# The first two blocks' front made in the projection's last token block, and the forget gates read one turn later

## What is computed

```python
h = rms_norm(x, norm_pre) * (1.0 + scale) + shift
q, k, v, f_logit, z_rwkv, p_pool, g = jnp.split(h @ w_in, IN_IDX, axis=-1)
# RWKV-7, before its scan over the tokens:
zf = zf + (token_shift(zf) - zf) * mu
r, k, v, wd, ad = jnp.split(zf, RWKV_IDX, axis=-1)
log_w = -DECAY_SCALE * jax.nn.sigmoid(w0 + jnp.tanh(wd) @ w2)
a = jax.nn.sigmoid(a0 + ad @ a2)
kk = (k * k_k).reshape(B, S, RWKV_HEADS, HEAD_DIM)
kk = kk / jnp.maximum(jnp.linalg.norm(kk, axis=-1, keepdims=True), 1e-12)
k = k * (1.0 + (a - 1.0) * k_a)
# attention: log_f = log_sigmoid(f_logit + f_bias), cum = cumsum(log_f)
y = jnp.concatenate([y_fox, y_rwkv, y_pool], axis=-1) * silu(g)
x = x + gate * rms_norm(y @ w_out, norm_post)
```

## Time and profile before

| | us |
|---|---|
| median of three runs | 3571.12 (3542.68 to 3572.24) |
| profiled execution | 3542.35 |
| its span | 3540.6 |
| TensorE matmuls busy | 3298.0 (93%) |
| VectorE busy | 2428.2 (69%) |
| ScalarE busy | 1965.7 (56%) |
| GpSimd busy | 1785.6 (50%) |

### The profile page before, as it was taken

One profiled execution on the slowest core, in us unless ns is written; L12 is line 12 of the kernel. 1 busy time (PEld: TensorE's weight loads), 2 busy tenths in 40 slices (PEclk: granted clock), 3 DMA queues, 4 the chain that ended last, 5 costly groups with the idle time before them and its releaser, 6 DMA issues. The chain is left out here.

```text
span 3540.6 us, 90103 instructions
## 1 busy us (share of the span) xinstructions
PE 3298.0 (93%) x31944; PEld 2282.0 (64%) x31944; DVE 2428.2 (69%) x4339; ACT 1965.7 (56%) x3745; POOL 1785.6 (50%) x2083
## 2 busy tenths in 40 slices
PE   6788999999999995999999899999999999979998
PEld 6783489459549742888888466566666666644444
DVE  5797756326533334788775889899899988965454
ACT  2444544325432234577774677677777777753333
POOL 2376400410230043254544798889889889852222
PEclk9898999999999997899998899999999999989999
DMA  7387435344444542232223202022020220215555
GB/s 317 129 303 254 167 128 190 131 149 159 159 143 152 169 155 82 63 86 79 65 53 74 52 16 59 10 56 59 9 58 10 57 58 7 60 70 190 188 185 178
DMA packets 247420, 401.09 MB, mean 113 GB/s; under 512 B 85549, under 2 KB 198916, under 8 KB 231844
## 3 DMA queue, kind: packets, MB, share of 16 engines
q1 hardware_dynamic: 223627, 383.75, 34.0%
q10 hardware_dynamic: 22880, 11.54, 1.3%
q0 software_dynamic: 480, 0.14, 0.1%
HBM read 272.77 MB, written 122.59 MB: 112 GB/s over the span
## 5 line engine op out<-in xcount | busy, mean ns | idle before, releaser
L2732 ACT ACTIVATE p<-psc,seam,sc 128x512 f32<-128x512 f32 (+3 forms) x1152 | 848.6, 743 | 283.1 <-PE psc L2793 270.2
L2711 POOL TENSOR_TENSOR plo<-p 128x512 f16<-128x512 f32 (+2 forms) x864 | 905.5, 1076 | 72.7 <-ACT p L2732 71.5
L2834 DVE TENSOR_REDUCE seam<-pm 128x1 f32<-128x512 f32 (+3 forms) x1152 | 703.5, 637 | 92.4 <-PE pm L1396 80.6
L646 PE MATMUL bank<-h,ring 128*128 128x512 f16 x2688 | 598.4, 381 | 4.5 <-DVE u L990 4.5
L651 PE MATMUL bank<-ring,h 128*128 128x128 f16 x8064 | 468.2, 222 | 25.5 <-ACT c L818 12.3
L646 PEld LDWEIGHTS bank<-h,ring 128*128 128x128 f16 x2688 | 264.1, 98 | 343.1 <-issue 43.0
L651 PEld LDWEIGHTS bank<-ring,h 128*128 128x128 f16 x8064 | 464.7, 99 | 27.0 <-issue 13.0
L1165 POOL CAST stage<-c 128x512 f16<-128x512 f32 x64 | 47.2, 738 | 767.5 <-DVE c L1006 767.5
L3036 PE MATMUL pz<-wo,yh 128*128 128x512 f16 x1024 | 305.6, 380 | 3.1 <-DVE yl L3068 3.1
L2864 DVE TENSOR_TENSOR plo<-p 128x512 f16<-128x512 f32 (+1 forms) x288 | 288.1, 1000 | 0.0
L1000 DVE TENSOR_TENSOR c<-bank,u 128x512 f32<-128x512 f32 x168 | 115.7, 689 | 249.3 <-PE bank L646 171.0
(11 more groups left out here) (430 smaller groups left out, 6837.2 us busy)
## 6 DMA issues: line engine op xcount, KB each, us to landing
ring<-scratch_ws SPq DMA_DIRECT2D x52, 1792.0 KB, 7.9
scratch_z<-stage SPq DMA_DIRECT2D x72, 256.0 KB, 3.1
scratch_ws<-h SPq DMA_DIRECT2D x10, 1792.0 KB, 6.9
y<-scratch_y SPq DMA_DIRECT2D x35, 512.0 KB
g<-scratch_g SPq DMA_DIRECT2D x35, 512.0 KB
xr<-in_x SPq DMA_DIRECT2D x34, 512.0 KB, 6.1
scratch_g<-stage SPq DMA_DIRECT2D x64, 256.0 KB, 6.2
scratch_qk<-stage SPq DMA_DIRECT2D x64, 256.0 KB, 2.6
```

Of the source, the lines that this page charges most:

```text
L646: t = nc.tensor.matmul(bank[b][:], m.ring[:, slot, l, bo, k, :], hh[:, side, r, ao, k, :], start=fresh and first, stop=last, skip_group_ch ...
L2711: nc.gpsimd.tensor_tensor(plo[:, k % NP, 0:w], p32[:, k % NP, 0:w], hi[:, 0:w], ALU.subtract)\
L2732: nc.scalar.activation(p32[:, k % NP, 0:w], psc[k % 2][:, 0:w], ACT.Exp, bias=xb[:, u, b, x // 4:x // 4 + 1], scale=m.sc[:, 0:1]).then_inc ...
L2834: nc.vector.tensor_reduce(mx[:, s, t, q:q + 1], pm[g][:, 0, 0:w], AX.X, ALU.max).then_inc(pm_d.sem, 1)
```

## The change

1. `h` is now two tensors, `h0` and `h1`. `h0` is kept to the attention's end, and the buffers of the front (before in `seam`) are carved from it, with `wa`, `vec` and two of the four buffers of `ar`; the other two of `ar` and `zv` are tensors of the recurrence.
2. The front's functions move, with their semaphores, into `block_front`, which both stages call. In the projection's last token block (turn FIRST = 297 opens it) the fronts of blocks 0 and 1 are made, beginning at turns FIRST + 29 and FIRST + 52. SP loads parameters and both z blocks in turn FIRST + 3. `logits` go to `ptr`, `kk_means` to `pf`.
3. `recur` makes fronts only for blocks 2 and up; `decay_sums` and the two matmuls before it come after the scores of block 0.
4. `forget` moves one turn on, behind the two last z shifts.

```diff
+        BEGIN = (29, 52)
+        def front_at(g, after):
+            r = g - FIRST - after
+            return BEGIN.index(r) if r in BEGIN[0:m.fronts] else None
...
@@ SP, project
+                    if g == FIRST + 3:
+                        sp.wait_ge(mm, FREE)
+                        fr.load_parameters(sp, a)
+                        for s in range(NC):
+                            sp.wait_ge(sent[s], 16 * (2 * TILES // NC))
+                        for b in range(m.fronts):
+                            fr.load_z(sp, b)
...
@@ TensorE, project, behind the turn's product
+                    b = front_at(g, 2)
+                    if b is not None:
+                        pe.wait_ge(m.f.par, 96)
+                        pe.wait_ge(f_out, NSB)
+                        if b:
+                            pe.wait_ge(m.f.gates_d.sem, b)
+                            pe.wait_ge(m.f.kss_d.sem, b)
+                        fr.logits(pe, b, (ptr[0][:], ptr[1][:]))
+                        fr.kk_means(pe, b, pf[:])
...
@@ ScalarE, project: tanh, kk_squares after 0 turns; gates, k_factor, norm_guard after 3; kk_inverse, exps after 6
+                    b = front_at(g, 5)
+                    if b is not None:
+                        fr.centred_sums(act, b)
+                        nc.scalar.preload_act_table_set(EXP_LN)
+                        fr.kk_log(act, b)
...
@@ VectorE, project: running_sums after 4, kk_unit after 7, operands after 8 (GpSimd: 5 and 8)
-                    if at is not None:
-                        if at[1] == 0:
-                            forget(at[0])
-                        elif at[2] == 1:
+                    if sub(g - 1) is not None and sub(g - 1)[1] == 0:
+                        forget(sub(g - 1)[0])
+                    if at is not None and at[1]:
+                        if at[2] == 1:
                             first_sum(at[0], at[1])
...
@@ recur, on each engine
-                    if there(n + 3):
-                        gates(n + 3)
+                    if FRONT <= n + 3 < BLOCKS:
+                        fr.gates(act, n + 3, bank)
...
@@ VectorE, recur
-                chain(nc.vector.memset(onesf[:], 1.0))
-                chain(nc.vector.memset(ls[:], 0.0))
-                decay_sums()
                 dve.wait_ge(cst, 2)
...
+                    if n == -2:
+                        decay_sums()
+                    if FRONT <= n + 3 < BLOCKS:
+                        fr.running_sums(dve, n + 3)
```

More of the change, by code:

```diff
@@ L1206, in _ @@
                         weight_sums(production(g, 0))
+                    b = front_at(g, 5)
+                    if b is not None:
+                        fr.k_new(pool, b)
+                    b = front_at(g, 8)
+                    if b is not None:
+                        fr.a_and_r(pool, b)
+                        fr.decay_between(pool, b)
+                        fr.r_k(pool, b)
 def persistent(nc, ctx):
@@ L1535, in recur @@
         pp_mm, pp_d = count("pp_mm", 1), count("pp_d", 1)
-        npar, nlate = 6, 11
+        nlate = 11
+        FRONT = m.fronts
         plan = m.plan
@@ L2075, in _ @@
                         state_decayed(n + 1, 0)
-                    if there(n + 4):
-                        tanh(n + 4)
-                        kk_squares(n + 4)
+                    if FRONT <= n + 4 < BLOCKS:
+                        fr.tanh(act, n + 4)
+                        fr.kk_squares(act, n + 4)
             @block.tensor
@@ L2124, in turn @@
                     g.then_inc(tr_mm.sem, 1)
-                def logits(b):
-                    past(pe, tanh_d, b, 1)
-                    past(pe, b_d, b - 1, 1)
-                    for k in range(2):
-                        for j in range(2):
-                            hs = rows(j)
-                            g = mm(bank[j][:, k * W:(k + 1) * W], wa[hs, k, :], zf[hs, b % 2, 4, :], start=True, stop=True)
-                    g.then_inc(wa_mm.sem, 1)
-                def kk_means(b):
-                    past(pe, ksq_d, b, 1)
-                    past(pe, b_d, b - 1, CB)
-                    mm(bank[2], m.headmean[:], ksq[:].rearrange("p k t -> p (k t)"), start=True, stop=True)\
-                        .then_inc(kk_mm.sem, 1)
                 def pool_product(b):
```

460 lines of the change are left out of this document (279 added, 181 removed).

## The result

The changed kernel takes 3537.3 us in the median of 20 runs (3517.2 to 3561.4), beside 3557.3 us for the kernel before in 20 runs of the same comparison (3542.7 to 3573.6). The ratio is 0.9937, with a 95% interval of 0.992 to 0.9954: 16 to 28 us less. The forecast was 3512 us. The measured time lies in its range (3494 to 3553), 25 us above its number. The profiled execution of the changed kernel took 3541.76 us (span 3540.1, mean granted clock 0.956), only 0.6 us less than that of before (3542.35 us).

The account below looks back on a forecast made before the run. TensorE bounds the projection; a chain through every engine and twice through HBM bounds the recurrence's first 90 us. Terms -7.2 - 6.2 + 4.4 - 21.4 = -30.4 from 3542.35 give 3512 us, range 3494 to 3553.

Parts of the forecast that it names:

- The stops, -7.2 us: Projection block starts: with forget gates later, three TensorE waits for copies shrink from 3.67 to 1.27 us, -7.2 us.
- The clock at these starts, -6.2 us: Three projection block starts: shorter stops leave TensorE's clock at 1.00, saving the slow stretches behind them, -6.2 us.
- The rival that the clock falls at the starts all the same (0.13): Projection block starts: clock still falls despite shorter stops, so 6.2 us are not gained, 3518 us; chance 0.13.
- Two fronts on TensorE, +4.4 us: Projection's last block: front matmuls for two blocks add 1.13 + 1.08 us each on TensorE, unhidden, +4.4 us.
- The rival of a front that waits for ScalarE (0.12): Projection's last block: a front matmul waits for ScalarE and the clock falls after it, +10 us, 3522; chance 0.12.
- The opening, -21.4 us: Recurrence's opening: block 0's scores start at once, so the chain through the first inverse ends earlier, -21.4 us.
- its rival: Recurrence's opening: HBM round trips run slower beside the loads, cutting the gain to 15 us, 3518 us; chance 0.10.
- The sum: Whole kernel: stops, clock, fronts and opening together, -7.2 - 6.2 + 4.4 - 21.4 = -30.4 us.
- What it was set against: Whole kernel: the sum was applied to the profiled execution's 3542.35 us, not the shown median of 3571.12 us.
- the lower as my number: Whole kernel: of two supposed run levels, the lower gives 3512 us; the upper, 3541 us, stays within the range.
- The slower rival's argument: Recurrence's first steps stay at low clock, 3552 us, chance 0.03; against it, clock returned after 16 us of solid work.

Follow-up runs that it names:

- e1: Kernel before with only the forget gates moved one turn later, behind the last z shifts; 3554.7 us, ratio 0.9979.
- e10: Changed kernel with 96 useless matmuls in recurrence steps 11 to 14, but only block 0's front made in the projection; 3513.9 us.
- e5: Kernel before with 96 matmuls of no use on TensorE in recurrence steps 11 to 14; 3538.1 us, ratio 0.9941.
- e2: Changed kernel with the forget gates put back at their old turn, so the fronts alone; 3533.7 us, ratio 0.9937.
- e4: Changed kernel with 96 matmuls of no use on TensorE in recurrence steps 11 to 14; 3507.3 us, ratio 0.9843.
- e3: Changed kernel run once more, unaltered, for a second profile; 3532.9 us, ratio 0.9924.
- e6: Changed kernel with 90 matmuls of no use on TensorE at the recurrence's opening, ahead of its first product; 3538.4 us, ratio 0.9933.
- e11: Changed kernel with 28 matmuls of no use, only at the small waits of recurrence steps 13 and 14; 3534.3 us.

## Why the prediction was off, by its own steps

- **The stops, -7.2 us: right.** Three waits of 1.3 us stand where three of 3.7 were.
- **The clock at these starts, -6.2 us: right, and 1.5 of it lost again elsewhere.** The clock is 1.00 at all three. In e1 the distances shrank by 3.5, 4.1 and 4.6 us, 12.2 in all, so 5.0 are the clock's where 6.2 were counted. (The second start was misread: by the earlier trace rows its slow stretch lasts from inside 786.5 to 787.0 to the end of 789.5 to 790.0, 3.4 us and not 2.9. With that, stop and clock make some 5.0, 4.1 and 4.7 us.) What is missing is at block 1, and it is the new fall at 630.4: 3.4 us at 0.50, which the prediction didn't have. All ten profiles with the later forget gates have one such fall of 3.4 us behind a wait of 2.0 us for the head means, and none of the four without them. In e10 it comes a block later (925.5), and there the first distance is 296.2, 4.9 us less than before, and the second 297.6. Why the same wait now tips the clock is open. The rival that the clock falls at the starts all the same (0.13) is out.
- **Two fronts on TensorE, +4.4 us: right.** The matmuls take 2.2 us each. From block 3 to the recurrence's first issue the fronts cost 5.1 us (291.7 against 287.5 to the set-up, the mean of before and e5, and the set-up lies 0.9 us closer to the first issue). The matmuls of the fronts wait for nothing; behind the second front a product's head means wait 0.9 us for ScalarE, once, which neither the kernel before nor e10 has. The 0.7 us at L897 is not the fronts': e2 doesn't have it. The rival of a front that waits for ScalarE (0.12) is out.
- **The opening, -21.4 us: right.** 86.7 to 64.9 us, so -21.8, and by the steps that it named. The first round trip took 7.6 us (1377.40 to 1385.03) where 6.9 were counted, and the second 7.2 where 7.5 were; the two nearly cancel, so the round trips were not slower by the 6 us of its rival. The prediction gave the rule of the Trainium skill ("TensorE: Matmul & The Clock Gate", "What's actually happening"), a low clock that activity releases, at most about 1 us here. The step is at 0.50 as before, so nothing was lost by it.
- **The sum: right within 3 us by the stages.** From block 1 to the first `right_side` the first pair of profiles gives -3.5 - 3.2 - 0.2 - 20.9 = -27.8, the pair with the fill (e5, e4) -28.3, beside -30.4. With the fill at the end, the medians of the two kernels differ by 30.8 us. Over the runs as they are it is less sharp: -20.0 by the medians of the first comparison and -24.2 in that of e3; both comparisons together give -25.5 by the means (20 to 31), and all 28 and 90 runs, on several chips, 3535.0 and 3562.3 us, -27.3 (22 to 32).
- **What it was set against: wrong, and this is the step that failed.** The prediction took the profiled 3542.35 us as one of two levels and gave "the lower as my number". The runs show no two levels. The 90 runs of the kernel before lie between 3541.8 and 3593.9 us, 31 of them between 3550 and 3565, with no gap wider than 2.3 us below 3585, and with the median at 3560.4; two of them are below 3543. The profiled run was close to the best draw that this kernel has. From the median, 3560.4 - 30.4 = 3530 would have been the number, and the changed kernel's 28 runs have their median at 3536.5. Of the 25 us by which the number was off, 15 are this (the kernel before has its median at 3557.3 us in the same comparison, not at 3542.35), and 10 are the gain's, 20.0 us there by the medians. Three runs and a profile stood ahead of the prediction, two of the runs 28.8 and 29.9 us above the profile; the forecast should have been a difference applied to their middle, not to the profile.
- **The slower rival's argument: wrong.** "After 16 us of solid work the clock was back every time" was true of the opening. In steps 13 to 15 both profiles of the changed kernel have some 100 us of nearly solid work at 0.50. This is why the two profiled times differ by 0.6 us: in the changed kernel's profile the part from step 12 to the last `ost` took 169.2 us, in that of before 147.6, so 21.6 of the 27.8 us are lost there (and 3.8 more ahead of block 1's marker, 480.7 and 484.5). It is a loss of that execution, as far as the runs tell, and not of the change: over the runs, the time at 0.50 worked out from the mean clock is 280 us for the changed kernel and 300 for the kernel before (70 runs), 20 less, which is what the starts and the opening account for in the first pair of profiles (14 and 7). Were the long stretch the change's own, the changed kernel would have more than the kernel before. That the two parts alone and the kernel before drew about 60 us there and both profiles of the whole 126 and 130 is five draws; the run of e6, the same kernel there, drew 96.
- **What no step had.** None of the named rivals came with its price. What moved the time was a cost that stood in the trace of before, 61 us at 0.50 from 1830 to 1985, and that the prediction never read, because the change doesn't touch it.

## What to carry to other kernels

A difference of profiles is only as good as the draw of the clock in each: subtract stages, not ends, and put the forecast on the median of the runs, never on the profile's own time. Where TensorE waits a few tenths of a microsecond between small matmuls in a chain of steps, look up the granted clock behind the waits; 96 matmuls of no use at the waits of four steps were worth as much as the whole change (-24.6 us to the kernel before, some -29 to the changed one, whose runs are of other chips), and the times spread less. At the opening a fill that stopped 5.5 us short of the work bought nothing; none that reached up to it was tried there.

## What the runs showed of the hardware

- TensorE's clock can stay at 0.50 for 130 us, with TensorE busy 18 to 20 of every 20 us for the first 100 of them, and come back or not behind the same rows: 34 us in one execution, 126 and 130 in two others. The work there is matmuls of 64 columns in fp32, and from 1918 us on also of 512 in fp16.
- In two profiles this fall comes behind waits of 0.45 and 0.69 us; with both filled (e11) the clock still fell, behind a wait of 1.46 us, so the small waits are not shown to be the cause. The Trainium skill ("TensorE: Matmul & The Clock Gate", "A second HAM failure mode: psum-queue depth-cycling") tells of a kernel in which short idles between groups of matmuls make the clock go up and down; these rows agree, with sizes.
- Behind one and the same wait of 2.0 us in the middle of block 1 the clock stayed at 1.00 in five profiles and fell for 3.4 us in nine (from 627 to 633 us on).
- A microsecond at 0.50 cost 0.37 us on the whole, less than the half that TensorE alone would lose. That other engines set the pace in part of that time is the likely reading; no run here separates it.
- The fill writes only to a PSUM bank that no other engine reads at its place: bank 4 ahead of the first product, the second chain bank behind `state`. The Trainium skill ("PSUM — Partial Sum Buffer", "Terms") states that two engines on one bank and the same partitions at once are an error, even where both only read; no run here shows it.
